# Taking the filler products of TensorE out of both attention stages of a two-layer encoder trunk

## The chip, the cores and the metric

The kernel runs on one core of one Trainium2 chip. The metric is the device time of one execution in microseconds (us), the median over several runs. Before the change it is 1315.49 us (three runs, 1313.08 to 1315.66).

## The reference, cut to what matters

Input and output are 256 tokens of 1024 numbers, float32. Layer 0 projects the normed tokens and runs two attentions beside each other: differential attention with 4 heads of two maps, and grouped-query attention with 8 heads, a window and sinks. Layer 1 runs a latent attention with 16 heads. Each is followed by an output projection, a norm and a feed-forward part: a dense SwiGLU in layer 0, the top 2 of 8 experts in layer 1.

```python
s = jnp.einsum('bqhd,bkhd->bhqk', qb, k).astype(jnp.float32) * scale
p = masked_softmax(s, chunk_causal_mask(b, seq))       # layer 1; blocks of 128 queries
w = p[:, :, 0] - lam * p[:, :, 1]                      # layer 0, differential heads
p = e / (jnp.sum(e, axis=-1, keepdims=True) + jnp.exp(sink - m))   # layer 0, window heads
x = x + (merged heads) @ w_out
```

The filler products are no part of this: their results are written to PSUM and never read.

## The kernel before, in words

The tokens lie in two tiles of 128 (`NT`). The dense weights come as a stream of pieces (`STREAM`) through a ring of six buffers. For each piece ScalarE rounds a high part (`w_hi`, L636 and L639), VectorE takes the low part (`w_lo`, L1053 and L1058), and TensorE makes three products for each pair of tiles (L1653 to L1655). Then the experts' weights go through 15 homes, each filled by SyncE (L450) when TensorE has used what was in it. No instruction order is planned at run time: each engine has its own list of instructions, written out by the program, and semaphores connect them.

Both attention stages are one function on each engine, called `attention`: with kind "AB" in layer 0 and with kind "C" in layer 1. A stage goes over 16 pairs of maps, two at a time, in eight steps i = 0 to 7. Steps 0 to 3 belong to the first tile of queries (128 keys), steps 4 to 7 to the second (256 keys). TensorE's order in a step is:

- `keep_clock` (L1657, called in L1782): the fillers, products of 128x128 by 128x512 from `hT_hi` into bank 2 (L1663). `FILL = (3, 1)` asks for three in each of the steps 0 to 3 and one in each of the steps 4 to 7, so 16 in a stage and 32 in all.
- `scores(i + 2)` (L1730), which waits until the exponentials of step i have been taken.
- `transposes(2i)` and `transposes(2i + 1)` (L1747): the probabilities are turned through PSUM.
- `values(2i)` and `values(2i + 1)` (L1772), which wait for the copies of the turned probabilities.

ScalarE's order in a step is: the two copies of the turned probabilities out of PSUM (L700), in layer 0 squares of the head outputs in two of the steps (L708), then the exponentials of step i + 2 (L687), and in steps 4 to 6 the high part of one piece of the next projection (L639). VectorE's order is: in layer 0 the combination of the two maps (L1160 to L1168), which the transposes of the differential heads wait for, then mask and maxima of the scores of step i + 2 (L1124 to L1140), which the exponentials wait for; after step 3 the merging of the first tile's heads (L1179 to L1186, in layer 1 L1189), in steps 5 to 7 the low part of a piece (L1058), and at the end the merging of the second tile.

After a stage TensorE transposes the merged tokens (L1674) and does the output projection. SyncE loads dense pieces when VectorE has made the low part of the piece six before, so loads follow from VectorE's progress.

The lines that matter in TensorE's list:

```python
for i in range(8):
    keep_clock(2, FILL[i // 4])
    if i + 2 < 8:
        scores(i + 2)
    transposes(2 * i)
    transposes(2 * i + 1)
    values(2 * i)
    values(2 * i + 1)
```

Of the kernel before, what the change touches and what calls it, by code (L numbers as in the profile page):

```python
# [15 lines left out]
P = 128  # L16
# [166 lines left out]


STREAM = IN0 + OUT0 + FFN + IN1 + UKV + UQ + OUT1
FILL = (3, 1)
SCAT_BANKS = (3, 4, 5, 7)
ADD_BANKS = (3, 4, 5, 7)
LAST_BANKS = (0, 1, 2, 6)
# [41 lines left out]
def build(nc, A):  # L231
# [3 lines left out]
    with ctx:  # L235
# [9 lines left out]
        def placed(name, shape, dt, k):  # L245
            return nc.alloc_sbuf_tensor_at(name, shape, dt, offset=SLAB + int(k * 4 * PIECE))
# [7 lines left out]
        hT_hi = placed("hT_hi", [P, KC, SEQ], f32r, 12)  # L254
# [85 lines left out]
        def bank(b):  # L340
            return PS[:, b, :]
# [277 lines left out]
        def _(a):  # L619
# [7 lines left out]
            def split_piece(u, n):  # L627

                a.wait_ge(ring_loaded[u % RING], 16 * (u // RING + 1))
                if u >= SLOTS:  # L630
                    a.wait_ge(used, u - SLOTS + 1)
                name, _, c0, c1, w = STREAM[u]
                if name in GAIN_AT:
                    for c in range(c0, c1):
                        o = (c - c0) * w
                        ins = a.activation(w_hi[:, u % SLOTS, o:o + w], ring[:, u % RING, o:o + w], ACT.Copy,  # L636
                                           scale=gains[:, GAIN_AT[name] + c:GAIN_AT[name] + c + 1])
                else:
                    ins = a.activation(w_hi[:, u % SLOTS, 0:n], ring[:, u % RING, 0:n], ACT.Copy)  # L639
                ins.then_inc(hi_ready, 1)  # L640
# [99 lines left out]
            for i, (_, n, c0, c1, w) in enumerate(IN0):  # L740
                def task():
                    q = IN0_ORDER.index(n)
                    for t in range(NT):
                        if q == 0:
                            a.wait_ge(rstd_ready, R_NORM0 + t + 1)
                        dst, src = z[:, t, n * COLS:n * COLS + w], bank((4 + 2 * q + t) % 8)[:, 0:w]
                        if n * COLS == ZB_Q:

                            dst = dst.rearrange("p (s m d) -> p m s d", s=4, m=2)
                            src = src.rearrange("p (m s d) -> p m s d", s=4, m=2)  # L750
                        evacuate(dst, src, stat[:, R_OFF[R_NORM0 + t]:R_OFF[R_NORM0 + t] + 1])
                    if q < 4:
                        a.wait_ge(evacuated, 2 * q + 2)
                        for t in range(NT):
                            if q:

                                a.wait_ge(ms_ready, R_QK0 + 2 * (q - 1) + t + 1)
                            m = IN0_HEADS[q] * HD
                            a.activation(sq[:, t * COLS:t * COLS + m], z[:, t, n * COLS:n * COLS + m], ACT.Square)\
                                .then_inc(squared, 1)  # L760
                    if q == 1:

                        a.wait_ge(lam_exp, 1)
                        a.activation(lam[:, 2:4], lam[:, 0:2], ACT.Exp).then_inc(lam_exp, 1)
                if 0 < i < len(IN0) - LATE:
                    split_ahead(i)
                if c1 == KC:
                    a.wait_ge(used, i + 1)
                    task()
# [880 lines left out]
        def _(pe):  # L1650
# [3 lines left out]
                pe.matmul(out, xh, wl, start=False, stop=False)  # L1654
                return pe.matmul(out, xl, wh, start=False, stop=stop)  # L1655

            def keep_clock(b, n):  # L1657

                for _ in range(n):
                    pe.matmul(bank(b), hT_hi[:, 0, 0:P], hT_hi[:, 0:2, :].rearrange("p c n -> p (c n)"),  # L1663
                              start=True, stop=True)

            def idle_clock(b, n):
                for _ in range(n):
                    pe.matmul(bank(b), idle[:, 0:P], idle, start=True, stop=True)
# [43 lines left out]
            def attention(s0, kind, between=None):  # L1712
                def scores(i):

                    t = i // 4
                    nk = P * (t + 1)
                    if i >= 2:

                        pe.wait_ge(exp_done, s0 + 2 * i - 2)
                    for s in range(2):  # L1720
                        p = 2 * (i % 4) + s
                        for m in range(2):
                            if kind == "AB":
                                r = slice(m * HD, (m + 1) * HD)
                                q = qkT0[r, p if p < 4 else 8 + p - 4, t * P:(t + 1) * P]
                                kk = qkT0[r, 4 + p if p < 4 else 12, 0:nk]
                            else:
                                q = qT1[0:C_QK, 2 * p + m, t * P:(t + 1) * P]
                                kk = kT1[0:C_QK, 2 * p + m, 0:nk]
                            ins = pe.matmul(bank(6 * (i % 2) + m)[:, s * SEQ:s * SEQ + nk], q, kk, start=True, stop=True)  # L1730
                    ins.then_inc(scored, 1)

                def transposes(i):
                    t, p = i // 8, i % 8
                    maps = 1 if kind == "AB" and p < 4 else 2
                    if maps == 1:

                        pe.wait_ge(probs_ready, 4 * t + p + 1)
                    else:
                        pe.wait_ge(exp_done, s0 + i + 1)  # L1740
                    if i >= 2:

                        pe.wait_ge(probsT_ready, s0 + i - 1)
                    for m in range(maps):
                        for b in range(t + 1):
                            j = m * (t + 1) + b
                            ins = pe.transpose(bank(2 + i % 2)[:, j * P:(j + 1) * P],  # L1747
                                               probs[:, i // 2 % 2, i % 2, m, b * P:(b + 1) * P], ident[:, :])
                    ins.then_inc(probs_transposed, 1)

                def values(i):
                    t, p = i // 8, i % 8
                    pe.wait_ge(probsT_ready, s0 + i + 1)
                    if i == 8:

                        pe.wait_ge(merged, s0 // 8 + 1)
                    maps = 1 if kind == "AB" and p < 4 else 2
                    for m in range(maps):
                        if kind == "AB" and p < 4:
                            out = bank(4)[:, p * P:(p + 1) * P]  # L1760
                            col, w = ZA_V + p * A_VD, A_VD
                        elif kind == "AB":
                            hd = p - 4 + 4 * m
                            out = bank(5)[:, hd * HD:(hd + 1) * HD]
                            col, w = ZB_V + m * HD, HD
                        else:
                            hd = 2 * p + m
                            out = bank(4 + hd // 8)[:, (hd % 8) * C_V:(hd % 8 + 1) * C_V]
                            col, w = hd * C_V, C_V
                        for b in range(t + 1):  # L1770
                            vv = (z if kind == "AB" else v1)[:, b, col:col + w]
                            ins = pe.matmul(out, probsT[:, i % 2, m * (t + 1) + b, :], vv,  # L1772
                                            start=b == 0, stop=b == t)
                    ins.then_inc(pv_done, 1)

                scores(0)
                if between is not None:
                    between()
                scores(1)
                for i in range(8):  # L1780

                    keep_clock(2, FILL[i // 4])  # L1782
                    if i + 2 < 8:
                        scores(i + 2)
                    transposes(2 * i)
# [3 lines that stand above are left out]
# [34 lines left out]
            pe.wait_ge(qkT_ready, 4)  # L1823
            pe.wait_ge(qkT_copied, 4)
            attention(0, "AB")
            transpose_h(lambda t: pe.wait_ge(merged, t + 1))

# [163 lines left out]
            for j in range(2):  # L1991
                for q in range(4):
                    c = 2 * q + j
                    ins = pe.matmul(PS[GROUP * q:GROUP * (q + 1), 4, 0:SEQ], rw_gained[:, c, :], x_cols[:, c, :],
                                    start=j == 0, stop=j == 1)
# [3 lines left out]
            for t in range(NT):  # L1999
                ins = pe.matmul(bank(5)[:, t * NE:(t + 1) * NE], logits_T[:, t * P:(t + 1) * P], fold,  # L2000
                                start=True, stop=True)
# [288 lines left out]
```

## Time and profile before

| | us |
|---|---|
| median of three runs | 1315.49 |
| the profiled execution's own time | 1309.51 |
| its span, first to last instruction | 1307.7 |
| TensorE busy | 1246.7 (95%) |
| VectorE busy | 461.2 (35%) |
| ScalarE busy | 356.9 (27%) |
| layer 0 attention, from the trace | about 74 to 118 |
| layer 1 attention, from the trace | about 378 to 424 |

The span is the time that the trace covers; the execution's own time is 1.8 us longer. Busy times are sums over the whole span. The granted clock of TensorE is the share of full speed (2.4 GHz) that the chip gave it: 1.00, or 0.50 (1.2 GHz). Its mean over the span is 0.989. In a timeline a row is a run of instructions of one line; the bracket tells how long the engine was idle before it and which instruction ended that.

### The profile page before, as it was taken

The page shows a single profiled execution, that of the slowest core. Times are in us where ns is not written, and L with a number is a line of the kernel's source. Part 1 is how long each engine was busy: PE and PEld are TensorE (multiplying, and loading weights), DVE is VectorE, ACT ScalarE, POOL GpSimd, SP SyncE. Part 2 cuts the span into 40 slices and gives each one's busy share as a digit, 9 for nine tenths or more (in the row PEclk, how much of TensorE's full clock was granted, in tenths as well). Part 3 has the DMA queues.
Part 4 walks back from the last instruction along what each step waited for, and adds up shares of the span by engine and source line. Part 5 has one row for each costly group of instructions (what it writes and reads, how often), then busy time and mean ns, then how long its engine had stood idle before and what let it go on. Part 6 is the DMA issues. An engine that isn't in the chain of part 4 may idle for free.

```text
span 1307.7 us, 22054 instructions
## 1 busy us (share of the span) xinstructions
PE 1246.7 (95%) x9542; PEld 618.5 (47%) x9542; DVE 461.2 (35%) x791; ACT 356.9 (27%) x706; POOL 58.2 (4%) x87
## 2 busy tenths in 40 slices
PE   7978999999868999999999999999999999999997
PEld 5756878888767733343333343332343333334332
DVE  5975655555565331131221132122122112312212
ACT  6456544454667210121100020011120011102101
POOL 4310000000330000000000000000000000000000
PEclk9999999999999999999999999999999999999999
DMA  9403445553502689989999999999999999999994
GB/s 345 164 26 117 173 161 193 193 187 118 190 35 97 278 317 374 390 341 421 421 420 421 420 420 420 420 405 409 420 420 421 420 420 420 421 420 401 390 420 199
DMA packets 58519, 413.55 MB, mean 316 GB/s; under 512 B 6832, under 2 KB 6976, under 8 KB 9008
## 3 DMA queue, kind: packets, MB, share of 16 engines
q1 hardware_dynamic: 57600, 411.20, 78.3%
q0 software_dynamic: 528, 0.79, 0.5%
q8 instruction: 77, 1.26, 0.4%
q14 instruction: 26, 0.21, 0.1%
q10 hardware_dynamic: 288, 0.08, 0.0%
HBM read 411.00 MB, written 1.05 MB: 315 GB/s over the span
## 4 chain that ended last, share of the span: by engine, by line
PE 87%; DVE 7%; ACT 3%; issue 1%; DMA 1%; POOL 0%; SPq 0%; ACTq 0%; DVEq 0%
PE PS L2142 39%; PE PS L2150 19%; PE PS L1653 6%; PE PS L1655 6%; PE PS L1654 6%; PE PS L2097 2%; DVE w_lo L1053 2%; PE PS L2049 2%; PE PS L2027 2%; PE PS L1772 1%; ACT arena L687 1%; DMA ring<-in_dense_tiles 1%; PE PS L1730 1%; ACT w_hi L636 1%; POOL stat L541 0%
## 5 line engine op out<-in xcount | busy, mean ns | idle before, releaser
L2142 PE MATMUL PS<-homes,arena 128*32 128x512 f32 x4704 | 515.9, 593 | 4.7 <-DVE arena L1592 4.7
L2142 PEld LDWEIGHTS PS<-homes,arena 128*32 128x32 f32 x4704 | 150.1, 110 | 344.4 <-issue 339.3
L2150 PE MATMUL PS<-homes,arena 128*32 128x512 f32 x2016 | 222.3, 592 | 0.0
L1588 DVE SCALAR_TENSOR_TENSOR arena<-arena,PS 64x512 f32<-64x512 f32 x63 | 42.8, 680 | 445.2 <-ACT arena L988 444.7
L1653 PE MATMUL PS<-w_hi,hT_hi 128*128 128x512 f32 (+2 forms) x372 | 143.5, 386 | 12.5 <-DVE w_lo L1053 7.6
L1655 PE MATMUL PS<-w_hi,hT_lo 128*128 128x512 f32 (+2 forms) x372 | 140.9, 379 | 0.0
L1654 PE MATMUL PS<-w_lo,hT_hi 128*128 128x512 f32 (+2 forms) x372 | 140.6, 378 | 0.0
L2150 PEld LDWEIGHTS PS<-homes,arena 128*32 128x32 f32 x2016 | 64.7, 110 | 146.9 <-issue 146.6
L1053 DVE SCALAR_TENSOR_TENSOR w_lo<-ring,gains,w_hi 128x512 fp32r<-128x512 f32 (+3 forms) x151 | 98.3, 714 | 49.8 <-ACT w_hi L636 49.7
L975 ACT ACTIVATE arena<-PS 128x512 f32<-128x512 f32 (+1 forms) x39 | 20.1, 515 | 350.3 <-PE PS L2097 350.0
L636 ACT ACTIVATE w_hi<-ring,gains 128x512 fp32r<-128x512 f32 (+3 forms) x151 | 92.0, 683 | 57.2 <-PE PS L1655 53.0
L988 ACT ACTIVATE arena<-PS 64x512 f32<-64x512 f32 x63 | 37.2, 590 | 255.6 <-PE PS L2142 255.6
L1653 PEld LDWEIGHTS PS<-w_hi,hT_hi 128*128 128x128 f32 x372 | 71.0, 191 | 29.1 <-DVE w_lo L1053 11.4
L1655 PEld LDWEIGHTS PS<-w_hi,hT_lo 128*128 128x128 f32 x372 | 70.9, 190 | 12.7
L1654 PEld LDWEIGHTS PS<-w_lo,hT_hi 128*128 128x128 f32 x372 | 71.2, 192 | 11.7
L1619 DVE TENSOR_TENSOR arena<-arena,PS 32x512 f32<-32x512 f32 x42 | 28.5, 679 | 89.2 <-ACT arena L1018 88.6
L1058 DVE TENSOR_TENSOR w_lo<-ring,w_hi 128x2048 fp32r<-128x2048 f32 x19 | 43.5, 2291 | 43.8 <-ACT w_hi L639 43.8
L1600 DVE TENSOR_TENSOR arena<-arena,PS 64x512 f32<-64x512 f32 x21 | 14.3, 679 | 125.1 <-ACT arena L1004 125.1
L1592 DVE SCALAR_TENSOR_TENSOR arena<-arena,PS 64x512 f32<-64x512 f32 x63 | 43.5, 691 | 2.0
L639 ACT ACTIVATE w_hi<-ring 128x2048 fp32r<-128x2048 f32 x19 | 36.5, 1922 | 23.6 <-PE PS L1655 23.6
L541 POOL TENSOR_TENSOR stat<-stat,neg_half 128x1 f32<-128x1 f32 (+4 forms) x24 | 33.5, 1406 | 166.7 <-DVE stat L1089 159.0
L2097 PEld LDWEIGHTS PS<-ident,arena 128*128 128x128 f32 (+2 forms) x188 | 26.0, 208 | 28.6 <-issue 24.3
(218 smaller groups left out, 930.5 us busy)
## 6 DMA issues: line engine op xcount, KB each, us to landing
homes<-in_expert_tiles SPq DMA_DIRECT2D x336, 1024.0 KB, 15.0
ring<-in_dense_tiles SPq DMA_DIRECT2D x50, 1024.0 KB, 4.8
ring<-in_dense_tiles SPq DMA_DIRECT2D x4, 512.0 KB, 3.3
ring<-in_dense_tiles SPq DMA_DIRECT2D x2, 832.0 KB, 4.2
x_res<-in_x SPq DMA_DIRECT2D x2, 512.0 KB, 4.2
out<-x_res SPq DMA_DIRECT2D x4, 256.0 KB, 3.1
ring<-in_dense_tiles SPq DMA_DIRECT2D x2, 256.0 KB, 6.8
rope<-in_rope POOLq DMA_DIRECT2D x2, 72.0 KB, 8.0
```

The source lines that it names most:

```text
L636: ins = a.activation(w_hi[:, u % SLOTS, o:o + w], ring[:, u % RING, o:o + w], ACT.Copy, scale=gains[:, GAIN_AT[name] + c:GAIN_AT[name] + c ...
L988: a.activation(gate[0:64, g, :], PS[0:64, g, :], ACT.Tanh, scale=0.5).then_inc(gate_ready, 1)
L1053: ins = v.scalar_tensor_tensor(out=w_lo[:, u % SLOTS, o:o + w], in0=ring[:, u % RING, o:o + w], scalar=gains[:, GAIN_AT[name] + c:GAIN_AT[ ...
L1058: ins = v.tensor_tensor(w_lo[:, u % SLOTS, 0:n], ring[:, u % RING, 0:n], w_hi[:, u % SLOTS, 0:n].bitcast(f32), ALU.subtract)
L1588: v.scalar_tensor_tensor(out=act_of[g], in0=gate[0:64, g, :], scalar=1.0, in1=PS[0:64, g, :], op0=ALU.add, op1=ALU.mult).then_inc(half_sil ...
L1592: v.scalar_tensor_tensor(out=act_of[g - 1], in0=act_of[g - 1], scalar=0.5, in1=PS[64:P, g - 1, :], op0=ALU.mult, op1=ALU.mult)\
L1653: pe.matmul(out, xh, wh, start=start, stop=False)
L1654: pe.matmul(out, xh, wl, start=False, stop=False)
L1655: return pe.matmul(out, xl, wh, start=False, stop=stop)
L2097: ins = pe.transpose(bank(b)[:, j * m:(j + 1) * m], cols[:, j % 2, :], ident[0:m, 0:m])
L2142: ins = pe.matmul(PS[GROUP * q:GROUP * (q + 1), g, :], xT[:, cc, o + g * GROUP:o + (g + 1) * GROUP], w[:, q * COLS:(q + 1) * COLS], start= ...
L2150: ins = pe.matmul(PS[GROUP * q:GROUP * (q + 1), 3 + g, :], tokens_T(k, c, q // 2, g), w[:, q * COLS:(q + 1) * COLS], start=k == 0 and c == ...
```

## The change

The constant `FILL` and the function `keep_clock` are taken out, and its call in the loop of the attention function on TensorE. Nothing else is touched. The other fillers, `idle_clock` at the start of the program and `token_clock` ahead of the experts, stay.

```diff
 STREAM = IN0 + OUT0 + FFN + IN1 + UKV + UQ + OUT1
-FILL = (3, 1)
 SCAT_BANKS = (3, 4, 5, 7)
...
-            def keep_clock(b, n):
-                for _ in range(n):
-                    pe.matmul(bank(b), hT_hi[:, 0, 0:P], hT_hi[:, 0:2, :].rearrange("p c n -> p (c n)"),
-                              start=True, stop=True)
...
                 scores(1)
                 for i in range(8):
-
-                    keep_clock(2, FILL[i // 4])
                     if i + 2 < 8:
                         scores(i + 2)
                     transposes(2 * i)
```

## Rows read from the trace of the kernel before

**Rows 1.** The page: the chain that ended last, by engine.

```profile
PE 87%; DVE 7%; ACT 3%; issue 1%; DMA 1%; POOL 0%; SPq 0%; ACTq 0%; DVEq 0%
```

**Rows 2.** The fillers' line: engine, operation, count, durations, first and last start.

```profile
L1663 PE MATMUL PS<-hT_hi x32: 390/436/774, 75.1 to 416.2; 128*128 128x512 f32 x32
```

**Rows 3.** Chain of waits, layer 1 attention: start us, us, what.

```profile
388.40 0.75 PE PS L1663 x3
...
400.40 0.28 PE PS L1663
...
405.53 0.29 PE PS L1663
...
416.42 0.53 PE PS L1663
```

**Rows 4.** ScalarE's timeline in layer 1 attention: start us, us, what, idle before.

```profile
389.50 0.21 ACT L687 ACTIVATION_READ_ACCUMULATOR arena<-PS,small,q_scale 128x1 f32 x1
390.30 0.66 ACT L700 ACTIVATE tabs<-PS 128x256 f32<-128x256 f32 x2 [0.59 <-PE PS L1747]
...
394.57 0.66 ACT L700 ACTIVATE tabs<-PS 128x256 f32<-128x256 f32 x2 [1.24 <-PE PS L1747]
...
398.85 0.66 ACT L700 ACTIVATE tabs<-PS 128x256 f32<-128x256 f32 x2 [0.28 <-PE PS L1747]
...
404.36 0.56 ACT L687 ACTIVATE arena<-PS,small,q_scale 128x256 f32<-128x256 f32 x1 [0.39 <-DVE small L1140]
...
417.84 0.60 ACT L700 ACTIVATE tabs<-PS 128x512 f32<-128x512 f32 x1 [1.47 <-PE PS L1747]
```

**Rows 5.** Chain of waits, layer 0 attention.

```profile
84.16 0.70 PE PS L1663 x3
...
110.14 0.53 PE PS L1663
```

**Rows 6.** Timelines of ScalarE and TensorE in layer 0 attention.

```profile
86.03 0.21 ACT L687 ACTIVATION_READ_ACCUMULATOR arena<-PS,small,q_scale 128x1 f32 x1
86.33 0.66 ACT L700 ACTIVATE tabs<-PS 128x256 f32<-128x256 f32 x2
...
111.56 1.29 ACT L700 ACTIVATE tabs<-PS 128x512 f32<-128x512 f32 x2 [0.88 <-PE PS L1747]
...
95.13 1.12 PE L1747 MATMUL PS<-ident,arena 128*128 128x128 f32 x4 [2.14 <-DVE arena L1168]
...
107.42 2.71 PE L1772 MATMUL PS<-arena,tabs 128*128 128x64 f32 x16 [2.57 <-ACT tabs L700]
```

**Rows 7.** Stretches: us, busy time of each engine, granted clock, DMA share, GB/s.

```profile
76.00:80.00 4.00, 1.38 (x11) 0.80 (x10) 2.98 (x12) 3.77 (x17) 0.00 (x0) 1.00 0.00 0
...
91.00:94.85 3.85, 1.99 (x15) 1.30 (x14) 3.58 (x10) 2.29 (x8) 0.00 (x0) 1.00 0.00 0
94.85:98.30 3.45, 3.12 (x13) 2.60 (x13) 3.10 (x11) 1.00 (x4) 0.00 (x0) 0.51 0.00 0
...
105.00:108.50 3.50, 1.08 (x10) 1.08 (x10) 1.52 (x1) 3.50 (x11) 0.00 (x0) 1.00 0.82 267
...
371.35:374.70 3.35, 2.75 (x13) 2.65 (x14) 3.25 (x6) 1.18 (x2) 0.95 (x1) 0.50 0.00 0
382.00:387.00 5.00, 3.44 (x23) 2.74 (x23) 2.78 (x9) 3.66 (x17) 1.93 (x5) 1.00 0.14 36
387.00:404.00 17.00, 15.69 (x98) 13.54 (x99) 8.14 (x19) 11.90 (x42) 0.00 (x0) 1.00 0.00 1
...
412.00:415.70 3.70, 1.72 (x16) 1.56 (x15) 2.00 (x1) 3.70 (x4) 0.00 (x0) 1.00 0.69 272
```

**Rows 8.** TensorE's timeline: sixteen transposes at the low and at the full clock.

```profile
371.95 3.28 PE L1961 MATMUL PS<-ident,h_tok 128*96 128x128 f32 x16 [5.61 <-DVE arena L1292]
...
379.29 1.91 PE L1961 MATMUL PS<-ident,arena 128*96 128x128 f32 x16
```

**Rows 9.** The stretch at the experts' start (columns of rows 7).

```profile
454.00:464.00 10.00, 9.76 (x85) 6.01 (x89) 8.82 (x49) 2.07 (x8) 0.00 (x0) 1.00 0.56 215
```

## The prediction

> **What bounds the kernel now.** I read the page's chain first: 87% of what ended last is TensorE [rows 1], so anything in TensorE's stream may be on the path. Then the fillers' own line: 32 products, and no other engine is recorded as waiting for them or they for it [rows 2]. So each is either in the way or fills a hole. The chain of waits tells the two apart. In layer 1 it runs through six groups of fillers: three of 0.75 us (one row stands for the three, which come once in each of the steps 1 to 3), 0.28, 0.29 and 0.53 [rows 3], 3.35 us in all. In layer 0 it runs through two: 0.70 and 0.53 us [rows 5]. The rest lie where TensorE would be idle: ahead of the transposes at 95.13 TensorE still waits 2.14 us for VectorE, ahead of the values at 107.42 it waits 2.57 us for ScalarE [rows 6], and between 76 and 80 it is busy only 1.38 of 4 us [rows 7].
>
> Being on the chain is an upper limit, since another engine may be close behind. Last I read the granted clock by stretches [rows 7], because the products taken out are also activity. The clock is 1.00 nearly everywhere and 0.50 (1.2 GHz) in short stretches. Two examples: TensorE was busy 1.99 of 3.85 us, with the last two microseconds empty, and then had 0.51; it was busy 1.08 of 3.50 and 1.72 of 3.70 us and the clock fell after both. So with the fillers in place the attention stages already stand near the edge.
>
> **The change part by part.** The edit adds no instruction and no wait; it moves none past a queue. Two effects are to be priced: the time given back, and the clock.
>
> *Layer 1, time given back at an unchanged clock.* The fillers of step 0 end before the exponentials that the next scores wait for: 0. Steps 1 to 3 have 0.75 us each [rows 3].
> - Step 1: the scores and transposes come 0.75 earlier, but ScalarE's copy at 390.30 had waited only 0.59 for the transposes (it was busy to 389.71) [rows 4]. Gain 0.59.
> - Step 2: the copy at 394.57 had waited 1.24 [rows 4], so the whole 0.75 comes through. Sum 1.34.
> - Step 3: the copy at 398.85 had waited 0.28 [rows 4]; the exponentials ahead of it have moved by the 1.34 already. Gain 0.28, sum 1.62.
> - Step 4: one filler of 0.28 [rows 3], and ScalarE's exponentials at 404.36 hang on VectorE's work behind those scores (0.39 idle) [rows 4]. I take 0.23 of it. Sum 1.85.
> - Steps 5 and 6: from 404.36 to 416.4 (the copy's start at 417.84 less its 1.47 idle) ScalarE takes exponentials, weight pieces and copies with no gap worth naming, and sets the pace [rows 4]. Gain 0 of 0.29.
> - Step 7: 0.53, at the low clock [rows 3]; the copy behind it waited 1.47 for the transposes [rows 4]. Gain 0.53. Sum 2.38.
>
> *Layer 0.* The 0.70 us at 84.16 come ahead of a copy at 86.33, but ScalarE was busy with exponentials to 86.24 [rows 5, 6]: gain 0.09. The others before 109 are covered by the waits for VectorE and ScalarE named above; if that cover went, they would be worth 0.7 (three) or 0.23 (one) each. In step 7 the copy at 111.56 waited 0.88 for transposes that stood behind a filler of 0.53 [rows 5, 6]: gain 0.53. Sum 0.62.
>
> Together 3.00 us. The bounds: 0 if every one is replaced by a wait just behind it, 3.35 + 1.23 = 4.58 if each chain piece is gained whole.
>
> *The clock.* Price: sixteen transposes take 3.28 us where the clock is low for nearly all of them and 1.91 at the full clock [rows 8], a ratio of 1.72. The low stretches in the trace last 3.4 us each. Where TensorE is the bound, one costs 3.4 - 3.4 / 1.72 = 1.42 us; where it has waits of its own, less, down to 0. How many are added the trace of before doesn't show. From below: none, and even less than none is possible, as the stretches now behind 108.5 and 415.7 fall on TensorE's path. From above: low all through, priced with the first rival. What I take is two. One at layer 1's entry: in 382 to 387 TensorE is busy 3.44 of 5 us [rows 7], 0.75 of them fillers; without them it is 2.7 of 5, or 0.54, hardly more than the 1.99 of 3.85, 0.52, that a fall followed. It costs 1.42, since from 387 TensorE is busy 15.69 of 17 us [rows 7]. The other in layer 0's first steps, where TensorE mostly waits: I take 0.2, near to 0, because in 76 to 80 TensorE is idle two thirds of the time even now [rows 7]. Together 1.6. Further on in layer 1 TensorE packs closer without fillers (each step of the first tile was 3.4 to 4.3 us and shrinks), so the share stays high and I take no more falls.
>
> Does the clock come back after each? After 371.35 TensorE had only transposes, busy 2.75 of 3.35 us at 0.50, and the clock was 1.00 again at 374.75 [rows 7, 8]. So the transposes of the attention stages seem to help to hold it. The Trainium skill, "TensorE: Matmul & The Clock Gate", section "Part 4: PE-mode transpose", says that transposes do not count as a busy TensorE in the same way and that the full clock doesn't engage for them. This trace disagrees for these float32 transposes; by the page's rule the attention stages would lose the share of activity that the transposes are, and the forecast would be the first rival's 1322.4 or more.
>
> *Sum:* -3.0 + 1.6 = -1.4 us. It passes to the end one for one: behind layer 0 stands a chain of TensorE's products, and at 454 to 464 the transfers run at only 0.56 of their capacity because the homes are full and wait for TensorE [rows 9]. The profiled execution would go from 1309.5 to 1308.1 us. The median of the runs shown is 6.0 us above this execution; so the forecast for the median is 1315.49 - 1.4 = 1314.1.
>
> **The rivals.**
> 1. *The low clock takes hold in attention (slower).* Without fillers about every second stretch is low. Layer 1's attention, 382 to 424, has room for 12 stretches of 3.4 us: six low against one now, 5 x 1.42 = 7.1. Layer 0's, 74 to 118, has room for 13: six against two now, at half the price since TensorE waits a third of the time, 4 x 0.7 = 2.8. With the 3.0 given back: +6.9, 1322.4. Low all through would be 11 x 1.42 + 11 x 0.7 - 3.0 = +20, 1336. It decides from the third added stretch at full price on (3.0 / 1.42 = 2.1), and can be measured from the fourth. For it: the falls now, with the fillers in. Against it: every fall was followed by a return after one stretch, once on transposes alone. A second way to the same price is that transposes hold the clock less than other products: 0.06 of this rival's 0.28. That is the rule of the Trainium skill's page named above.
> 2. *The clock stays as it is (faster).* All of the 3.0 is kept: 1312.5. For it: 15.69 of 17 us busy in layer 1. Against: layer 0's first steps get emptier.
> 3. *The gain is swallowed (no change).* If not TensorE but the experts' transfers set the end, and if they start as before, nothing arrives: 1315.5. Against it: those transfers wait for the same stage's pieces.
>
> **How the numbers follow.** About 0.2%, 2.6 us, is what a measurement of this kernel can tell from no change. Forecast case 0.43 (of it 0.05 faster, 0.36 within, 0.02 slower), rival 1 0.28 (slower), rival 2 0.19 (0.16 faster, 0.03 within), rival 3 0.10 (within). That gives faster 0.21, within 0.49, slower 0.30. The range goes from the full 4.2 us gain (near the 4.58 bound), 1311.3, to 1325, past rival 1's centre by some two stretches; what is left out is mostly rival 1's upper part.
>
> **What would show it.** In the changed trace: L1663 gone; in layer 1's first tile the values following each other in about 2.8 us steps instead of 3.4 and more; the copies of ScalarE there waiting 0.3 us or less; layer 0's attention the same length to within 1 us. For the clock: a low stretch near 385 and one near 78, and the full clock in between. It is wrong if more than four low stretches are added (then rival 1), or if the stage shortens and the end doesn't move (rival 3).

## The result and the profile after

Five runs of the changed kernel have a median of 1322.06 us (1318.72 to 1326.61), five of the kernel before 1315.49 (1313.05 to 1318.65). The ratio is 1.0059, 95% interval [1.0035, 1.0083]: the change makes the kernel slower by 0.35 to 0.83%. The forecast was 1314.1 with "within 0.2%" as the likeliest; rival 1 stood at 1322.4.

| | profiled, before | profiled, after |
|---|---|---|
| own time of the execution | 1309.51 | 1321.44 |
| mean granted clock | 0.989 | 0.970 |
| layer 0 attention: first scores to first product of the next projection | 43.6 | 47.6 |
| of it at 1.2 GHz | 6.8 | 29.7 |
| layer 1 attention, the same | 45.1 | 51.1 |
| of it at 1.2 GHz | 3.4 | 23.9 |
| rest of the span | 1219.0 | 1220.9 |

The stage lengths are differences of start times in TensorE's timeline, the time at 1.2 GHz is from the granted clock's records. Of the 11.9 us between the two spans 10.0 lie inside the two stages. From the first product of layer 1's output projection to the experts' first product it is 35.8 us in both traces, and the experts' products take 835.1 us in both: what a stage loses reaches the end whole.

The page of the kernel after, the span and the row of TensorE's clock in 40 slices:

```profile
span 1319.6 us, 21990 instructions
...
PEclk9977999999987999999999999999999999999999
```

It was all nines before. Slices 3 and 4 are layer 0's attention, 12 and 13 layer 1's. The stretches of the kernel after show what TensorE did before and during the low clock (from and to, us; busy time of TensorE, of its weight loads, VectorE, ScalarE, GpSimd, each with its number of instructions in brackets; granted clock, DMA share, GB/s):

```profile
75.00:78.85 3.85, 0.89 (x18) 0.70 (x14) 2.37 (x7) 2.02 (x9) 0.00 (x0) 1.00 0.00 0
78.85:89.00 10.15, 9.71 (x43) 6.77 (x44) 7.24 (x26) 7.42 (x35) 0.00 (x0) 0.50 0.01 2
...
106.00:109.50 3.50, 0.38 (x4) 0.14 (x2) 1.63 (x4) 3.50 (x9) 0.00 (x0) 1.00 0.42 115
109.50:123.20 13.70, 13.25 (x59) 12.43 (x60) 8.49 (x12) 6.89 (x16) 1.01 (x1) 0.50 0.55 202
...
389.40:392.80 3.40, 1.60 (x12) 1.36 (x12) 1.45 (x6) 3.40 (x17) 0.42 (x2) 1.00 0.09 22
392.88:409.95 17.07, 16.68 (x58) 14.23 (x59) 3.85 (x12) 8.08 (x30) 0.00 (x0) 0.50 0.00 1
```

Read them in pairs: a stretch with holes at 1.00, then the stretch that follows it. The falls come after holes, as before the change [rows 7]. What is new is the second row of each pair. The low clock now lasts 10, 14 and 17 us, and all that time TensorE is busy 96 to 98%. In before's trace each low stretch in the two stages ended after 3.4 us. The number of falls in the two stages went from three to five; two of the five, at 78.85 and 392.88, are new and stand at the stages' entries. The last row answers to 387 to 404 of before, 17 us with 98 records of TensorE's products at full clock [rows 7]; now the same length holds 58.

The chain of waits in layer 1 (start us, us, what), where three fillers stood in each of these steps [rows 3]:

```profile
393.18 1.97 PE PS L1762 x8
395.15 1.81 PE PS L1720 x8
396.96 0.44 PE PS L1737 x2
397.43 0.39 ACT tabs L699
397.86 1.97 PE PS L1762 x8
399.83 3.52 PE PS L1720 x8
```

L1762, L1720 and L1737 are the values, scores and transposes. Eight products of the values took 1.10 us before, and the scores from 399.83 took 1.73. A step from values to values is 4.68 us here and 6.39 in the next; with fillers they were 3.45 and 4.27.

### The profile page after: what moved, and what is told of

It reads as the page before. It is cut to its first block, busy times and chain, and to the rows that moved or that the text cites. A ratio compares the mean times of both kernels' runs of the same rounds, so it can differ in the third digit from the quotient of the medians.

```text
span 1319.6 us, 21990 instructions
## 1 busy us (share of the span) xinstructions
PE 1260.0 (95%) x9510; PEld 632.2 (48%) x9510; DVE 461.6 (35%) x791; ACT 357.7 (27%) x706; POOL 58.2 (4%) x87
## 4 chain that ended last, share of the span: by engine, by line
PE 88%; DVE 6%; ACT 3%; issue 1%; DMA 1%; POOL 0%; SPq 0%; ACTq 0%; DVEq 0%
PE PS L2130 38%; PE PS L2138 19%; PE PS L1652 6%; PE PS L1653 6%; PE PS L1654 6%; PE PS L2085 2%; PE PS L1762 2%; PE PS L2037 2%; PE PS L2015 2%; DVE w_lo L1052 2%; PE PS L1720 1%; ACT arena L686 1%; DMA ring<-in_dense_tiles 1%; PE PS L1664 1%; ACT w_hi L635 1%
## 5 line engine op out<-in xcount | busy, mean ns | idle before, releaser
L1762 PE MATMUL PS<-arena,tabs 128*128 128x64 f32 (+1 forms) x168 | 32.3, 361 | 9.7 <-ACT tabs L699 9.4
```

## The experiments

Theory 1: the whole loss is low clock in the attention stages, which begins in TensorE's holes and, without fillers, doesn't end when TensorE is busy again. Rivals: the loss sits in one stage, or is an accident of one trace; it is TensorE's streaming time that counts and not what streams; the number of fillers over a stage matters and not their place. Each kernel was timed beside the kernel before on one chip. Stage lengths are from each run's own profile, so from one execution each.

| run | ratio to before, 95% interval | median us | median clock | layer 0 stage (at 1.2 GHz) | layer 1 stage (at 1.2 GHz) |
|---|---|---|---|---|---|
| e1_only_layer0 | 1.0029 [1.0008, 1.0049] | 1319.46 | 0.975 | 46.4 (20.5) | 51.1 (23.9) |
| e2_only_layer1 | 1.0026 [1.0005, 1.0046] | 1319.00 | 0.975 | 48.5 (30.7) | 45.1 (3.4) |
| e3_quarter_rows | 1.0173 [1.0156, 1.019] | 1337.24 | 0.962 | 55.4 (47.8) | 57.6 (30.1) |
| e4_double | 1.0021 [1.0008, 1.0034] | 1318.52 | 0.984 | 48.2 (10.2) | 50.7 (10.2) |
| e5_transposes | 0.9981 [0.9964, 0.9998] | 1313.06 | 0.982 | 45.6 (17.1) | 44.7 (3.4) |
| e6_gaps | 0.9942 [0.9924, 0.996] | 1307.12 | 0.989 | 42.6 (0) | 41.4 (0) |
| e7_gaps_and_path | 0.9963 [0.9948, 0.9979] | 1309.31 | 0.989 | 42.6 (0) | 43.9 (0) |
| e8_gaps_no_entry | 0.9993 [0.9976, 1.0009] | 1313.71 | 0.983 | 44.6 (9.3) | 48.6 (17.1) |
| e9_entry_alone | 0.9985 [0.9973, 0.9996] | 1312.01 | 0.977 | 47.2 (30.0) | 41.4 (0) |
| e10_gaps_and_heads | 0.9958 [0.9942, 0.9974] | 1309.85 | 0.990 | 42.6 (0) | 41.4 (0) |
| e11_both_entries | 0.9987 [0.9972, 1.0002] | 1312.65 | 0.978 | 48.3 (30.1) | 44.7 (9.9) |
| e12_gaps_again | 0.9946 [0.9929, 0.9962] | 1307.62 | 0.988 | 42.6 (0) | 41.4 (0) |

The kernel before had medians of 1313.8 to 1315.1 us and a median clock of 0.981 beside them.

### Which stage: e1 and e2

```diff
-                    keep_clock(2, FILL[i // 4])
+                    keep_clock(2, FILL[i // 4] if kind == "AB" else 0)    # e1; kind == "C" in e2
```

e1, expected:

> Fillers stay in layer 0's attention and are gone from layer 1's. Theory 1 (the loss is low clock, in both stages, about 4 us of stage length in layer 0 and 6 in layer 1): layer 0's stage is as long as before the change (about 43.6 us from its first scores to the first product of the next projection) with some 7 us of low clock; layer 1's has some 15 to 30 us of low clock and is longer by 3 to 6 us than with fillers (45.1 us). Time 1317 to 1321. Theory 2 (the loss sits in layer 0 alone, and layer 1's difference is an accident of this one trace): the time equals that of the kernel before within 2 us.

e2, expected:

> Fillers stay in layer 1's attention and are gone from layer 0's. Theory 1: layer 0's stage is 2 to 4 us longer than 43.6, with 20 to 30 us of low clock; layer 1's is as before. Time 1316 to 1320; the two halves' losses add up to the whole change's 6.6 us. Theory 2: all of the 6.6 us, 1322.

Both halves lose: 0.29% and 0.26%, together 0.55% against 0.59% for the whole. Theory 1 holds and the loss in one stage falls. Layer 1's stage was 51.1 us in e1 as in the changed kernel, and 45.1 in e2 as before. Layer 0's stage in e1 is a warning: the same instructions as before took 46.4 us there and not 43.6, with 20.5 us at 1.2 GHz and not 6.8. The expectation missed this, and e2's had layer 0's stage 2 to 4 us longer than 43.6, where it is 4.9; that stage varies from execution to execution. The four profiled executions without fillers or with the entry's alone in layer 0 (after, e2, e9, e11) have 29.7 to 30.7 us low there and 47.2 to 48.5 us of length, against 6.8 and 20.5 us low and 43.6 and 46.4 us of length with the fillers of before, so the two kinds still lie apart.

e1 also limits theory 1. Its layer 0 has the fillers of before, and the clock fell at 79.94, behind the hole of 2.07 us that before's trace has at the same place. It stayed low for 10.2 us, as long as in the changed kernel. TensorE's timeline of e1 just before and in that stretch:

```profile
79.77 1.11 PE L1730 MATMUL PS<-arena 64*128 64x128 f32 x8 [2.07 <-ACT arena L687]
...
82.73 1.63 PE L1663 MATMUL PS<-hT_hi 128*128 128x512 f32 x3
...
87.16 1.63 PE L1663 MATMUL PS<-hT_hi 128*128 128x512 f32 x3
```

So three fillers in a step did not bring the clock back sooner at that entry. Further on in layer 0 the theory holds better: the low stretches there are 3.4 us each with fillers (two in before, three in e1), and without them the longest is 10.2 us in e2, 13.7 in the changed kernel and 17.1 in e9 and e11.

### What holds the clock: e3, e5 and e4

e3 gives each filler 32 rows of the array in place of 128, with the same 512 columns. e5 puts two transposes in each filler's place. e4 doubles the fillers.

```diff
-                    pe.matmul(bank(b), hT_hi[:, 0, 0:P], hT_hi[:, 0:2, :].rearrange("p c n -> p (c n)"),
+                    pe.matmul(bank(b), hT_hi[0:32, 0, 0:P], hT_hi[0:32, 0:2, :].rearrange("p c n -> p (c n)"),  # e3
...
+                    for q in range(2):                                                                        # e5
+                        pe.transpose(bank(b)[:, q * P:(q + 1) * P], hT_hi[:, q, 0:P].bitcast(f32), ident[:, :])
...
-FILL = (3, 1)
+FILL = (6, 2)                                                                                                 # e4
```

> All 32 fillers stay, with the same columns and so the same time on TensorE's stream, but over 32 rows of the array in place of 128. Theory 1a (the clock follows how much of the array works): the clock falls nearly as without fillers, and the fillers' time is paid on top, so 1322 to 1326. Theory 1b (it follows how long TensorE streams, whatever the rows): as the kernel before, 1315 within 2 us, mean clock 0.985 or more. Theory 3 (the fillers' worth has nothing to do with the clock): as before too, but then with a clock like that without fillers.

> Each filler product (512 columns, 0.23 us in the stream) is replaced by two transposes of 128 by 128, about 0.22 us in the stream. If transposes count as activity like other products (as the return of the clock after 371.35 in the kernel before suggests): as the kernel before within 2 us, mean clock 0.985 or more. If they do not count (the rule of the Trainium skill, TensorE: Matmul & The Clock Gate, Part 4: PE-mode transpose): the clock falls as without fillers, 0.965 to 0.975, and the time is 1322 to 1325, as their own time is paid too.

> Twice the fillers, six and two in a step. If the clock is held all through, the added 32 products cost 0.23 us each where TensorE's stream is on the path: layer 1's steps 1 to 3 get 0.7 us longer each, about 2.5 to 3.5 us in all, less what the vanished low stretches give back (up to 2). Time 1315 to 1318. If instead each removed filler were worth its time and the loss came from elsewhere, the same 3.5 us, and no change in the low stretches.

e3 settles that streaming time alone doesn't hold the clock. TensorE was at least as long in the fillers as before (median 623 ns each, before 436), and the clock was low for 47.8 of 55.4 us in layer 0. The stretches of that run, one for each stage:

```profile
78.20:133.60 55.40, 49.41 (x204) 36.05 (x205) 32.49 (x80) 32.00 (x107) 2.02 (x2) 0.57 0.17 58
394.30:451.90 57.60, 52.56 (x256) 43.91 (x257) 23.79 (x45) 32.45 (x89) 2.74 (x6) 0.74 0.17 58
```

The time lies 11 us above the expectation's upper end. The direction was right, the price was not: the two stages are 7.8 and 6.4 us longer than in the changed kernel. I had put the fillers at 0.23 us each, but 20 of the 32 start at 1.2 GHz, where one takes 0.43. 20 x 0.43 + 12 x 0.23 = 11.4 us would be their own time if all were on the path; the clock was also low for 24.3 us longer than in the changed kernel (18.1 and 6.2). No run separates the two.

e5 went against the rule of the Trainium skill that its expectation names ("TensorE: Matmul & The Clock Gate", "Part 4: PE-mode transpose"). Transposes in the fillers' place hold the clock (0.982, before 0.981), and the kernel is if anything a little faster than with the fillers. So float32 transposes count as activity here. The expected mean clock of 0.985 or more was too high for both kernels.

e4 came out just above the expected 1315 to 1318. More fillers at the same places raise the mean clock only from 0.981 to 0.984: 10.2 us of each stage were still at 1.2 GHz, while the added products lengthened both stages. The holes at the two entries shrank (2.07 to 1.38 us, 1.28 to 0.60), but holes of 1.91, 2.27 and 2.35 us further on in layer 0 and of 1.98 us in layer 1 stayed, and behind the last of these the clock was low for 10.2 us, with two fillers in the step. Between the holes of layer 0 three added fillers made a step 0.7 us longer (4.46 in place of 3.76), so they were on the path there.

### Fillers where TensorE waits: e6 and e12

```diff
+LEAD = {"AB": (8, 3, 3, 3, 0, 0, 0, 0), "C": (8, 0, 0, 0, 0, 0, 0, 0)}
+GAP_T = {"AB": (0, 0, 0, 0, 7, 0, 0, 0), "C": (0, 0, 0, 0, 0, 0, 0, 0)}
+GAP_V = {"AB": (0, 0, 0, 0, 0, 8, 8, 0), "C": (0, 0, 0, 0, 0, 0, 7, 0)}
...
-                    keep_clock(2, FILL[i // 4])
+                    keep_clock(2, LEAD[kind][i])
                     if i + 2 < 8:
                         scores(i + 2)
+                    if GAP_T[kind][i]:
+                        pe.wait_ge(merged, s0 // 8 + 1)
+                        keep_clock(5, GAP_T[kind][i])
                     transposes(2 * i)
                     transposes(2 * i + 1)
+                    keep_clock(5, GAP_V[kind][i])
                     values(2 * i)
```

> Fillers only where TensorE waits anyway: eight in step 0 of both stages, three in steps 1 to 3 of layer 0, seven ahead of the transposes of step 4, eight ahead of the values of steps 5 and 6 in layer 0, seven ahead of the values of step 6 in layer 1; none ahead of layer 1's scores in steps 1 to 5 and none in step 7. Theory 1: no low clock in either stage (the 6.8 us in each are gone), layer 1's stage 2 us shorter than 45.1 and layer 0's 1 to 2 us shorter than 43.6: time 1311 to 1313. If the scores of layer 1 need fillers beside them in steps 1 to 3, low clock appears there and the time is 1315 to 1318.

> The run with fillers in the gaps once more, beside the other kernels' chip, since the later run with fourteen more came out slower against its own runs of before. If the first result holds: ratio to the kernel before 0.993 to 0.996 and no low clock in the two stages. If its 0.9942 was luck in the clock outside the stages: 0.996 to 0.998.

This beats both kernels: 0.58% and, in a second sample, 0.54% faster than before. Neither trace has any low clock in the two stages. That doesn't hold for every execution: e8 has e6's instructions in layer 0, and its trace has 9.3 us of low clock there, from 110.64 on; and three of e6's ten executions stood at a mean clock of 0.983 to 0.985 and 1310.7 to 1311.5 us. In layer 1 it takes 15 fillers, one fewer than before, and its stage is 41.4 us in place of 45.1. TensorE's timeline of e6 there (start us, us, what, idle before), with the hole ahead of the scores filled:

```profile
381.89 2.06 PE L1665 MATMUL PS<-hT_hi 128*128 128x512 f32 x8
384.13 1.16 PE L1732 MATMUL PS<-arena 96*128 96x128 f32 x8 [0.18 <-ACT arena L689]
...
386.16 1.10 PE L1774 MATMUL PS<-arena,tabs 128*128 128x64 f32 x8 [0.44 <-ACT tabs L702]
...
388.91 1.10 PE L1774 MATMUL PS<-arena,tabs 128*128 128x64 f32 x8 [0.26 <-ACT tabs L702]
...
392.49 1.10 PE L1774 MATMUL PS<-arena,tabs 128*128 128x64 f32 x8 [0.26 <-ACT tabs L702]
```

The steps are 2.75 and 3.58 us, each 0.7 shorter than before. The gain, 7.2 us between the medians, is more than the expectation's 2 to 4. Measured against before's profiled execution the two stages are only 1.0 and 3.7 us shorter. Measured against e1's layer 0, the same instructions as before's in another execution, the first is 3.8 us shorter, and 3.8 + 3.7 = 7.5.

### The path's price and the entry: e7, e8, e9, e11

```diff
 e7: LEAD "AB": (8, 3, 3, 3, 0, 0, 0, 1), "C": (8, 3, 3, 3, 1, 1, 0, 1); the gaps as in e6
 e8: LEAD "C": (0, 0, 0, 0, 0, 0, 0, 0); all else as in e6
 e9: LEAD "C": (8, 0, 0, 0, 0, 0, 0, 0); no other filler in either stage
e11: as e9, with LEAD "AB": (8, 0, 0, 0, 0, 0, 0, 0)
```

> The run with fillers in the gaps, with the fillers on the path put back: three in steps 1 to 3 of layer 1, one in its steps 4, 5 and 7 and in step 7 of layer 0. The clock is high through both stages in either, so the difference is the time of the products on the path alone. The prediction's sum for it was 2.4 + 0.6 = 3.0 us with step 7 at the low clock; at the full clock 0.23 in place of 0.53 twice, so 2.4. Expected: layer 1's stage 41.4 + 2.1 = 43.5 us, the time 1309.5. If the earlier gain was the placement and not the products taken off the path: 1307 again.

> The run with fillers in the gaps, without the eight ahead of layer 1's step 0. Theory 1: the clock falls at layer 1's entry and, because a step of narrow products at 1.2 GHz does not bring it back, stays low for 10 us or more with TensorE nearly always busy; layer 1's stage is 46 to 49 us instead of 41.4, the time 1311 to 1314. Rival (the prediction's own step: a fall is followed by a return after one stretch of 3.4 us): 41.4 + 1.4 = 43 us, the time 1308.5.

> The changed kernel with eight fillers put back, all ahead of layer 1's step 0, none anywhere else. Theory 1: layer 1's stage is 42 to 45 us (low clock only near its end) instead of 51.1, layer 0's as in the changed kernel. Time 1314 to 1317, so eight products recover most of what thirty-two did. Rival (the number of fillers over the stage matters): 1320 to 1322.

> The changed kernel with eight fillers ahead of step 0 in both stages, sixteen in all. If layer 0 loses its time the same way as layer 1 (one fall at the entry that then lasts), layer 0's stage goes from 47 us to 43 to 44, and the time is 1308 to 1310. If layer 0 has several holes of its own (its steps 4 to 7 wait 2 us and more for VectorE and ScalarE), the entry alone changes little: its stage stays at 45 to 47 us, the time 1310 to 1312.

e7 against e6 prices the fillers on the path at the full clock: layer 1's stage 43.9 against 41.4, so 2.5 us, and layer 0's 42.6 in both, so its one filler in step 7 costs nothing there. The timeline of e7 shows the same products as e6's above, with the fillers back:

```profile
385.90 1.10 PE L1774 MATMUL PS<-arena,tabs 128*128 128x64 f32 x8 [0.43 <-ACT tabs L702]
386.81 0.94 PE L1665 MATMUL PS<-hT_hi 128*128 128x512 f32 x3
...
389.34 1.10 PE L1774 MATMUL PS<-arena,tabs 128*128 128x64 f32 x8 [0.26 <-ACT tabs L702]
390.25 0.94 PE L1665 MATMUL PS<-hT_hi 128*128 128x512 f32 x3
```

e8 and e9 are the sharpest pair. With eight fillers missing at layer 1's entry the stage goes from 41.4 to 48.6 us; with these eight alone in the changed kernel it is 41.4 again and not 51.1. Without them (e8's timeline, TensorE):

```profile
388.80 1.16 PE L1732 MATMUL PS<-arena 96*128 96x128 f32 x8 [1.99 <-ACT arena L689]
389.80 0.60 PE L1749 MATMUL PS<-ident,arena 128*128 128x128 f32 x4
390.84 1.97 PE L1774 MATMUL PS<-arena,tabs 128*128 128x64 f32 x8 [0.44 <-ACT tabs L702]
392.60 2.02 PE L1732 MATMUL PS<-arena 96*128 96x128 f32 x8
```

A hole of 0.94 us ahead of the scores at 385.68 and one of 1.99 us ahead of these, and from 390.5 to 407.6 everything runs at half the clock. In e9, from 393 to 410, the granted clock is 1.00 with no filler among the products:

```profile
393.00:410.00 17.00, 15.69 (x105) 13.79 (x104) 7.74 (x18) 13.67 (x49) 0.00 (x0) 1.00 0.00 1
```

So the same stream of scores, transposes and values keeps a high clock high and a low one low. The rival in e8's expectation, a return after one stretch, falls. The profiled execution of e8 is the second slowest of its twelve (1318.49 us; they run from 1309.88 to 1320.1, with mean clocks of 0.988 down to 0.976), so by their clocks the faster ones had less of it low. e9 came out faster than expected, 1312.0 in place of 1314 to 1317 us; its stage in layer 1 had no low clock even at its end, which the expectation had left room for.

e11 limits this. Layer 0 gained nothing from its entry's fillers (48.3 us, 30.1 of them low, more than the 45 to 47 us expected). The clock fell there three times, at 84.1, 101.2 and 108.0. Ahead of the last two stand holes of 2.43 and 2.12 us; ahead of the first TensorE had only shorter ones, of 0.53 and 0.93 us, and was busy 2.23 of 3.39 us:

```profile
80.70:84.09 3.39, 2.23 (x20) 1.41 (x16) 3.10 (x14) 2.42 (x12) 0.00 (x0) 1.00 0.00 0
```

And in e11 layer 1 was low again at its end, after the hole that the seven fillers of e6 close:

```profile
414.00:418.60 4.60, 2.52 (x24) 2.29 (x22) 2.61 (x3) 4.60 (x8) 0.00 (x0) 1.00 0.58 194
418.60:428.80 10.20, 10.20 (x49) 9.72 (x49) 6.03 (x8) 4.12 (x7) 0.31 (x1) 0.50 0.58 222
```

e9 had the same hole and no fall. The two kernels have the same instructions in layer 1, so whether such a hole costs anything differs from execution to execution.

### A miss: e10

```diff
+                if t == 0:
+                    keep_clock(0, 14)
                 pe.wait_ge(qk_normed, 7 + t)
```

> The run with fillers in the gaps and fourteen more in the hole of 5.6 us ahead of layer 1's query transposes. Sixteen of these transposes took 3.28 us at the low clock and take 1.91 at the full one; VectorE's norm of the second tile runs beside them, so 0 to 1.4 us are gained. Time 1306 to 1307. If the fillers start at the low clock and run over the hole (14 at 0.43 are 6.0 us): 1307 to 1308.

It took 1309.85 us and not 1306 to 1308. The bank that the fourteen write is free only when VectorE has copied the keys out of it, and that took most of the hole. TensorE's timeline of e10:

```profile
374.03 6.16 PE L1665 MATMUL PS<-hT_hi 128*128 128x512 f32 x14 [4.28 <-DVE arena L1294]
380.02 1.91 PE L1966 MATMUL PS<-ident,h_tok 128*96 128x128 f32 x16
```

The fillers waited 4.28 us, ran at 1.2 GHz (0.43 us each) and pushed the transposes back. The clock was back for these (1.91 us in place of 3.23 in e6), but from the end of the keys' transposes to the stage's first scores it took 14.8 us, in e6 12.0. These 2.8 us are as much as the medians differ by. Across the two chips that difference is not clear of noise: the ratios, 0.9958 and 0.9942, have intervals that overlap.

## Why the prediction was wrong

The step that failed is the question "Does the clock come back after each?". I had read from before's trace that each low stretch ended after 3.4 us, once on transposes alone, took that for a property of the clock, and priced each added fall as 3.4 us of low clock, 6.8 us in all. In the two profiled executions it was 43.4 us more (53.6 against 10.2). The number of falls was right: "What I take is two", one at each entry, and two were added, there. What was wrong is how long a fall lasts: 10.2, 6.8, 13.7, 17.1 and 6.8 us in the changed kernel, so those that were there before grew too. e8 and e9 show that in layer 1 the scores, transposes and values alone don't bring a low clock back for 17 us, though TensorE is busy 98% of the time. The return on transposes didn't repeat either: in the changed kernel the stretch from 375.81, transposes alone again and TensorE busy 5.75 of 6.80 us, lasted 6.8 us and not 3.4. Nor do fillers assure a short stretch: e1 had one of 10.2 us at layer 0's entry and e4 one at layer 1's end, with fillers in. I had also taken the closer packing without fillers as a reason for no more falls. For falls that was right (e9: none while the steps pack closely). It says nothing of the return.

Point by point:
- **Where the fillers are on the path**: right for layer 1 (2.5 us between e7 and e6). In layer 0 the step-7 filler was given 0.53 us, or 0.23 at the full clock; e7 and e6, which differ there in that filler alone, have 42.6 us both. Whether the other fillers of layer 0 are covered at the full clock is open, as no run without them kept the full clock there.
- **The time given back**: right in size for layer 1. The sum had 0.59 and 0.75 us for steps 1 and 2; e6 shows 0.70 and 0.69. For all of layer 1 at the full clock the sum was 2.1 and the measurement 2.5 us. The 0.62 us of layer 0 no run shows.
- **The price of low clock**: right in layer 1. Without fillers its stage is 51.1 us with 23.9 of them low and, in e9, 41.4 with none low, where only the eight fillers in a wait are added: 9.7 over 23.9 is 0.41 per us, or 1.4 per 3.4 us, and I had 1.42. In layer 0 the full clock's 42.6 us (e6) is the nearest stand-in: 4.9 over 29.7 is 0.17 per us, or 0.6 per 3.4 us, an estimate; rival 1 had half the price, 0.7, and the forecast 0.2 for its one stretch.
- **How much low clock**: wrong, as told. With rival 1's count, 5 and 4 more stretches, its sum of +6.9 us met the measured +6.6 between the medians. That was rival 1 with 0.28 and should have been the forecast. That the two numbers lie so close is in part luck: between the profiled executions it was the time of seven (layer 0) and six (layer 1) more stretches, and the difference was 11.9 us, because the execution of before was a fast one.
- **The way to the end**: right, one for one; rival 3 falls.
- **The rule on transposes**: the trace's row was the better guide on whether they count, and e5 confirms that they do. The forecast would have been near the measured time by the Trainium skill's rule, but for a wrong reason.

A second fault lay in the starting point. The profiled execution of before stood 6.0 us below the median, and I carried that along as an offset. Over 98 further executions of the kernel before, the median clock is 0.981 and a straight line through time against clock gives about 0.3 us for each us at 1.2 GHz (correlation 0.91). The execution I read had 0.989 and 1309.5 us, a higher clock and a shorter time than any of the 98 (0.985 and 1310.45 at best). It had 10.2 us of low clock in the two stages; layer 0's stage alone had 20.5 in e1 with the same instructions, 10.2 of them in one stretch. A trace like e1's would have shown that a low stretch can last longer than 3.4 us.

## What to carry to other kernels

Before taking fillers out, ask two separate questions of the granted clock: whether the clock falls in the stream that is left, and how long it stays low once it has fallen; here the second decided the price. Put fillers into the waits that the timeline names, ahead of the instruction that waits, and none beside work that fills TensorE already: here that was worth over 0.5% against the kernel before and, by way of it, over 1% against the changed one, with 55 fillers in place of 32. A stage at the edge of the clock differs between executions of the same program, so compare the profiled execution's own time and mean clock with those of the other runs before reading a price from it.

## What the runs showed of the hardware that I had not expected

- The low clock can last under load. TensorE was busy 16.68 of 17.07 us at 0.50 in the kernel after; the same products at 1.00 in e9 stayed there.
- What streams counts as well as how long. Fillers over 32 of the array's rows, with the same columns, left the clock low for 47.8 of 55.4 us in layer 0; over 128 rows it was low for 6.8 and 20.5 us in two executions.
- Activity beside the attention's products doesn't always end a low stretch: it lasted 10.2 us at layer 0's entry with three fillers in a step (e1) as without any (after).
- Float32 transposes hold the clock as well as the products they replaced (e5: median clock 0.982 against 0.981).
- Why e9 and e11 differ at the same hole near layer 1's end (no fall, and 9.9 us low) stays open, and so does why the same instructions in layer 0 had 6.8 us low in one execution and 20.5 in another.
